# Moving two projections, the low-rank product and the head sums at the end of a hybrid decoder's token tiles

## What is computed

```python
h = _rmsnorm(x, norm_pre[l])
c = _split_cols(h @ w_in[l])
log_a = jax.nn.log_sigmoid((c['a_lr'] @ gla_w_a2[l] + gla_b_a[l]).astype(F32)) / GATE_NORM
o_a, s_gla_new = _chunked_gated_linear(heads(q_a), heads(c['a_k']), heads(c['a_v']), heads(log_a), s_gla)
o_a = (_head_rmsnorm(o_a, gla_norm[l]) * jax.nn.silu(c['a_z'])).astype(dt)
u_b = c['b_c'] * c['b_v']
conv = sum(ext_b[:, j:j + T] * conv_w[l, j] for j in range(CONV_W))
o_b = (c['b_b'] * conv * jax.nn.silu(c['b_z'])).astype(dt)
o_c, s_hgrn_new = _chunked_gated_linear(heads(q_c), heads(k_c), heads(c['c_i']), heads(log_f), s_hgrn)
o_c = (_head_rmsnorm(o_c, hgrn_norm[l]) * jax.nn.silu(c['c_z'])).astype(dt)
mix = jnp.concatenate([o_a, o_b, o_c, o_d], axis=-1)
x = x + _rmsnorm(mix @ w_out[l], norm_post[l])
```

## Time and profile before

| | |
|---|---|
| time, median of 3 runs | 1055.08 us (1049.93 to 1057.19) |
| time of the profiled execution | 1054.02 us |
| its span in the profile | 1052.2 us |
| PE busy | 997.0 us, 95% of the span |
| DVE busy | 652.7 us, 62% |
| ACT busy | 422.6 us, 40% |
| POOL busy | 388.5 us, 37% |
| mean granted TensorE clock | 0.985 of full speed |

### The profile page before, as it was taken

The page is one execution under the profiler, slowest core; times in us unless marked ns, Lnnn a source line. Parts: engine busy times, 40 slices in busy tenths (PEclk is TensorE's granted clock), DMA queues, the critical chain, the costliest instruction groups (busy, mean ns, idle before and its releaser), DMA issues.

```text
span 1052.2 us, 27303 instructions
## 1 busy us (share of the span) xinstructions
PE 997.0 (95%) x11696; PEld 739.7 (70%) x11696; DVE 652.7 (62%) x1356; ACT 422.6 (40%) x829; POOL 388.5 (37%) x534
## 2 busy tenths in 40 slices
PE   3997889999999999999999999999999999999997
PEld 3755777855887667865887668865787667867774
DVE  5987788645755558545755567546656467537564
ACT  6862363531533334432534333432534324333414
POOL 2453732174305550174305650174304650155310
PEclk9996899999999999999999999999999999999999
DMA  9820352001110021001110021001210021001011
GB/s 321 283 77 2 104 170 66 21 2 41 62 61 1 2 83 60 21 2 42 62 61 1 2 84 59 21 2 41 62 61 1 2 82 61 2 1 42 2 63 45
DMA packets 30747, 57.29 MB, mean 54 GB/s; under 512 B 2673, under 2 KB 17819, under 8 KB 30619
## 3 DMA queue, kind: packets, MB, share of 16 engines
q1 hardware_dynamic: 30627, 55.55, 15.8%
HBM read 45.78 MB, written 9.86 MB: 53 GB/s over the span
## 4 chain that ended last, share of the span: by engine, by line
PE 66%; DVE 20%; DMA 5%; ACT 5%; issue 3%; SPq 1%; DVEq 0%; ACTq 0%
PE pj L726 29%; PE op L950 15%; PE pj L745 9%; PE sc L827 5%; DVE A L1945 2%; DMA xin<-in_x_prompt_t 2%; DMA xin<-in_x_prompt 2%; DVE w_lo L1831 1%; DVE h_lo L1859 1%; DVE xin L1846 1%; DVE X L2133 1%; PE op L970 1%; DVE X L2139 1%; PE m L884 1%; PE sc L838 1%
## 5 line engine op out<-in xcount | busy, mean ns | idle before, releaser
L726 PE MATMUL pj<-h_hi,w_hi 128*128 128x256 f16 (+1 forms) x1728 | 211.8, 266 | 2.3 <-DVE w_lo L1831 1.7
L726 PE MATMUL pj<-h_lo,w_hi 128*128 128x256 f16 (+1 forms) x1728 | 209.8, 265 | 0.0
L726 PE MATMUL pj<-h_hi,w_lo 128*128 128x256 f16 (+1 forms) x1728 | 209.5, 265 | 0.0
L1945 DVE COPY_PREDICATED A<-cu,sc 64x128 f32<-64x128 uint8 x384 | 131.9, 343 | 104.7 <-PE sc L827 98.6
L532 POOL TENSOR_TENSOR G<-B 128x256 f32<-128x256 f32 x112 | 79.7, 712 | 312.5 <-DVE B L1880 167.0
L726 PEld LDWEIGHTS pj<-h_hi,w_hi 128*128 128x128 f16 x1728 | 152.4, 99 | 29.9 <-issue 5.2
L726 PEld LDWEIGHTS pj<-h_lo,w_hi 128*128 128x128 f16 x1728 | 158.8, 99 | 17.5
L726 PEld LDWEIGHTS pj<-h_hi,w_lo 128*128 128x128 f16 x1728 | 158.6, 99 | 17.4
L543 POOL TENSOR_TENSOR G<-G,Q 128x256 f32<-128x256 f32 x112 | 86.0, 768 | 99.1 <-issue 70.8
L1373 ACT ACTIVATE G<-G 128x512 f32<-128x512 f32 x112 | 69.0, 621 | 62.0 <-POOL G L533 61.3
L544 POOL TENSOR_TENSOR G<-G,K 128x256 f32<-128x256 f32 x112 | 93.4, 834 | 0.0
(11 more groups left out here) (289 smaller groups left out, 1389.3 us busy)
## 6 DMA issues: line engine op xcount, KB each, us to landing
xin<-in_x_prompt SPq DMA_DIRECT2D x17, 512.0 KB, 4.3
wo_hi<-in_w_units SPq DMA_DIRECT2D x16, 512.0 KB, 5.2
xres<-in_x_prompt SPq DMA_DIRECT2D x15, 512.0 KB, 4.3
xin<-in_x_prompt_t SPq DMA_DIRECT2D x14, 512.0 KB, 4.1
out_y_prompt<-xres SPq DMA_DIRECT2D x14, 512.0 KB, 2.8
wo_lo<-in_w_units SPq DMA_DIRECT2D x12, 512.0 KB, 6.0
xres<-in_w_out SPq DMA_DIRECT2D x8, 256.0 KB, 3.3
gpost<-in_w_out SPq DMA_DIRECT2D x8, 256.0 KB, 4.0
```

Of the source, the lines that this page charges most:

```text
L726: m = pe.matmul(b[:, j * T:(j + 1) * T], w[:, k, col + 128 * j:col + 128 * j + 128], h[:, k, :], start=(n == 0 and k == 0), stop=(n == 2 a ...
L1945: m = dve.copy_predicated(out, mk.unsqueeze(1).broadcast_to([64, 4, 32 // h, h]), half(SC[hh], u)[:, 0:128].rearrange("p (q b w) -> p q b ...
```

## The change

In the steady tiles the order of helper calls changes on three engines; no instruction is added or taken out. On PE the projection b_b moves in front of `updates(i, 1)`, so that two projections (b_v and b_b) stand there; `low_rank(i + 1)` moves up to stand right behind `updates`; `recall(i, 1)` moves behind b_z; and `head_sums(i, 1)` stands between the two halves of c_z. On ACT `square(i, 1)` moves behind `gate_log(i, "B")`, and `gate_sigmoid(i, "B")` in front of `inv_rms(i, 1)`. On DVE `alpha_sum(i + 1)` moves behind `gate_min(i, "B")`. The branches `if i < NT ... else` inside the loop go too; since i ends at NT - 1, their else parts never ran.

```diff
                 proj(i, "b_v")
+                proj(i, "b_b")
                 updates(i, 1)
-                proj(i, "b_b")
+                low_rank(i + 1)
+                proj(i, "b_z")
                 recall(i, 1)
-                if i < NT:
-                    low_rank(i + 1)
-                else:
-                    tails_out(i)
-                proj(i, "b_z")
-                if i < NT:
-                    log_alpha(i + 1)
-                else:
-                    out_section(0, 0)
-                    out_section(0, 1)
+                log_alpha(i + 1)
+                proj(i, "c_z", (0,))
                 head_sums(i, 1)
-                proj(i, "c_z")
+                proj(i, "c_z", (1,))
...
                 keys_out(i, 1)
-                if i < NT:
-                    x_hi(i + 1, 1)
-                square(i, 1)
-                if i < NT:
-                    low_rank_out(i + 1)
-                else:
-                    tails_store(i)
+                x_hi(i + 1, 1)
+                low_rank_out(i + 1)
                 gate_in(i, "B")
                 gate_log(i, "B")
-                if i < NT:
-                    alpha_log(i + 1)
+                square(i, 1)
+                alpha_log(i + 1)
+                gate_sigmoid(i, "B")
                 inv_rms(i, 1)
-                gate_sigmoid(i, "B")
                 mix_hi(i, "B")
...
                 gate_abs(i, "B")
-                if i < NT:
-                    alpha_sum(i + 1)
                 gate_min(i, "B")
+                alpha_sum(i + 1)
                 normalise(i, 1)
```

## The result

The changed kernel takes 1066.45 us (median of 4 runs, 1065.45 to 1068.46) against 1052.54 us for the kernel before in the same job (4 runs, 1049.93 to 1057.19). The ratio is 1.013, 95% interval 1.0084 to 1.0176: slower by some 13 to 14 us. The forecast was 1065.6 us in a range of 1056 to 1070. Measured a second time, beside the experiments, it was 1.0123 (1.0088 to 1.0158).

The account below looks back on a forecast made before the run. The prediction took PE, busy 95% of the span, as the bound. From 1054.0 us it added 6.6 for longer tiles, subtracted 1.45 at a_k and added 6.4 for clock falls: 1065.6 us, range 1056 to 1070.

Parts of the forecast that it names:

- What is taken away: PE, six steady tiles: updates no longer waits for ACT's copy of the keys, 0.8 x 6 = 4.8 us.
- What is late next: PE, six steady tiles: low_rank waits for x_lo on DVE, whose end stays put, 1.9 to 3.1 us each.
- I take this at nothing: DVE: states(i, 1, 0) kept waiting by the later updates, taken as zero; other bound a few tenths per tile.
- Recall out of the shade: PE behind b_z: recall no longer fills a wait, 1.1 us per tile (0.9 to 1.2), 6.6 us in six.
- The tail: Tile end: splitting c_z costs nothing; forget_in 0.25 us later, but a_k's hidden wait disappears, giving back 1.45 us.
- The clock: TensorE behind the new gaps: granted clock falls to half in four of six tiles, 6.4 us (0 to 9.8).
- The sum: Whole kernel: 1054.0 + 6.6 - 1.45 + 6.4 = 1065.6 us.
- One of my own signs: Steady tiles: one not 0.8 us or more longer would refute low_rank's new wait for x_lo.
- the clock holds: Rival, steady tiles: same stalls without clock falls, 1059.2 us; chance 0.30, including one or two falls.
- The stall is really gone: Rival, PE: x_lo comes some 2.3 us earlier and both waits vanish, 1047.1 us; chance 0.08.
- The gate chain takes over: Rival, gate B to a_k: gates lose over 0.8 us, a_k waits again, about 1069 or 1072 us; chance 0.07.
- It changes nothing: Rival, score products: PE's 5.7 us of waits for DVE shrink by what comes late, 1055 us; chance 0.05.

Follow-up runs that it names:

- the kernel that does only that: Kernel before with keys_out in front of mix_hi A on ACT, nothing else moved: 1055.78 us, ratio 1.0014.
- The kernel with b_b back: Changed kernel with b_b put back behind updates, the rest of the change kept: 1061.73 us, ratio 1.0061.
- the tail's: Kernel before with only head_sums between the halves of c_z and the change's moves on ACT and DVE: 1055.29 us, ratio 1.0005.
- The filled gap: Changed kernel with 16 more 128x256 matmuls that nobody reads between updates and low_rank: 1061.03 us, ratio 1.0057.
- the second profile of the changed kernel: Changed kernel run again without any edit, against the kernel before: 1067.16 us, ratio 1.0123.
- Two edits of which neither alone shows a gain: Kernel before with convolution in front of x_scale on DVE (alone 0.9996) and keys_out in front of mix_hi A on ACT (alone 1.0014); together 1047.21 us, ratio 0.9918.

## Why the prediction was right, and where it was off

**What is taken away: right.** `updates` waits no more, 4.8 us in six tiles. That taking this wait away doesn't pay by itself is shown by the kernel that does only that: 1.0014.

**What is late next: right in kind, short on one edge.** The new wait sits where forecast, in six tiles; I had 1.9 to 3.1 us each and 14 in all, the list has 12.3. The step that I left out is the bank: b_b fills the bank that `conv_gate` on ACT has to read first, so b_b itself starts 0.29 us late (414.41 to 415.57 for a step of 0.87). Before, `updates` and its wait stood in between. Six times that is 1.7 us, and with 12.3 it makes the 14. That the total agrees so closely is in part luck, because the single waits don't: the spread that I read from the tiles of the kernel before (1.9 to 3.1) is gone in all but tile 5.

"I take this at nothing" was the other slip: four of the six waits are 1.87 us to the hundredth, and tile 3's row shows why. `updates` comes late enough that the states wait for it, and from there to `low_rank` the way is fixed: states, `x_lo`, signal. So in five of the six tiles (not in tile 5) the last thing that the states wait for is no longer DVE's run behind the DMA but PE's own lateness. It costs little, because the two end close together: beyond the usual step of 0.13 us the states wait 0.14, 0.04 and 0.16 us in tiles 2 to 4 and almost nothing in the others, some 0.4 us in all. Against my statement that nothing of this moves, the mechanism has changed; against the other bound that I gave, a few tenths per tile, the size is smaller still.

**Recall out of the shade: right, at the upper bound.** 1.1 us was the term and 1.2 its bound "with another small gap in front of it". From the start of `low_rank` to that of c_z the changed kernel takes 8.08 us in tiles 2, 4 and 7, where the clock held. The kernel before takes 7.73 in tile 3 (421.72 to 429.45), of which 0.87 are `head_sums`, which now stands later: 6.86. The difference is 1.21 us: `recall`'s 1.03, 0.1 in front of it (b_z takes 5.34 for 5.25) and 0.1 behind it (`log_alpha` 0.97 for 0.87). Six times that is 7.3 us, not 6.6. The kernel with b_b back less the tail's, 1061.73 - 1055.29 = 6.4 us, is near what this gives for it, 7.3 lost less the 5 x 0.3 won in front of a_k, 5.8.

**The tail: right.** It costs nothing that can be measured, and the hidden wait of a_k comes back as soon as PE is on time. In the changed kernel's profile 0.19 us of it is left in one tile of five, so some 1.3 of the 1.45 us came back.

**The clock: right, one fall fewer.** I took four falls of 1.6 us. The first profile has three, the second four; in tile 3, b_z's 7.01 us less 5.25 less the 0.1 us gap in front of `recall` is 1.7. The Trainium skill, "TensorE: Matmul & The Clock Gate", Part 1, has the slow clock as the state to which an idle array returns. The filled gap agrees in kind: with 1.75 us of work that nobody needs, 1.00 in all six tiles.

**The sum.** By spans, 1065.3 - 1052.2 = 13.1 us, and it closes by stretches. At tile 2's `low_rank` the changed run is 1.1 us later (303.23 against 302.12). Of this 0.98 us is there at the start of b_v (289.82 against 288.84), in front of the first place where the two programs differ: it isn't the change but the difference of two executions. The other 0.1 is the states' wait. From there to tile 7's `low_rank` the run takes 606.8 us (303.23 to 910.02) for 596.0 (302.12 to 898.16), 10.8 more: `recall` 5 x 1.21 = 6.1, three falls 5.0, a_k back -1.3, and 0.7 at the score products, whose waits are 7.8 us in twelve where the same stretch of the kernel before has 7.1 in eleven (the earlier trace rows begin behind two of these). That makes 10.5, and 0.2 more are what the states wait for `updates` in tiles 3 to 7. The last 1.2 us are tile 7's `recall`.

So the change itself costs 12.1 us in these two profiles, where my sum had 11.6. The sum was short by 0.7 at `recall`, 0.4 at the states, 0.2 at a_k and 0.7 at the score products, which it had at nothing (they may be scatter: the second profile of the changed kernel has 6.7 us there, in eleven). It was long by 1.4 at the clock, nearly all of it the one fall. These slips nearly cancel, so that 1065.6 lies within 1 us of the median is partly luck; the mechanism and each term, to within 1.5 us, are not.

One of my own signs came out against me. I wrote that a steady tile not 0.8 us or more longer would refute the stall. From tile 2's `low_rank` to tile 3's the changed kernel takes 120.24 us for 119.60, 0.64 more. But the same distance in the kernel before runs from 118.18 to 119.60 by itself, so a single tile can't carry that sign; the five together, 10.8 us, can.

Of the rivals, "the clock holds" gave 1059.2 and is the case of the kernel with b_b back and of the filled one, at 1061 to 1062; the 2 us more are of the size of the slips above without the clock. "The stall is really gone" fell with h_lo's row. "The gate chain takes over" fell with the tail alone. "It changes nothing" fell with the result.

## What to carry to other kernels

A wait in the profile names the releaser that came last, and the next one may be tenths of a microsecond behind it. Before moving work to hide a wait, write down when each later input of that engine can be ready, and which piece of independent work is now covering the difference: here `recall` covered a wait that the list showed as only 0.4 us. Where a run on another engine sets the date, shorten that run and remove the first wait together; here neither alone showed a gain. Then ask what starts that run: here it was a DMA that waited for the same engine to free its buffer. And keep the waits of TensorE apart: two of 0.8 and 1.2 us cost their length, one of 1.9 us could cost 1.7 us on top.

## What the runs showed that I had not expected

- TensorE's clock fell in dense work too. Gaps of 1.87 us, with 0.6 us of small matmuls in front of them (`updates`) and 0.75 us behind (`low_rank`), in work that is otherwise full 128x128 matmuls, brought it to half for about 3.4 us in some tiles and not in others, in another set of tiles in the next execution; the gap of tile 5, the longest, 2.93 and 3.72 us, brought it in both. The shortest wait behind which it fell was 1.85 us; waits of up to 1.67 us in tiles 2 to 7 never brought it, in any of the twelve profiles.
- Work that nobody reads made the kernel faster: 96 more matmuls, about 7 us less.
- Two edits of which neither alone shows a gain (1.0014 and 0.9996) are together worth 0.8%.
